# Opening of a two-block kernel: x loaded by feature columns instead of token rows, the first norm's sums made by TensorE and its factor multiplied in by GpSimd

## What is computed

```python
def rmsnorm(x, g):
    y = xf * lax.rsqrt(jnp.mean(xf * xf, axis=-1, keepdims=True) + RMS_EPS)
    return (y * g).astype(x.dtype)

cond = jax.nn.silu(c)
mod = (cond @ ada_w[i] + ada_b[i])[:, None, :]
sh1, sc1, g1, sh2, sc2, g2 = jnp.split(mod, 6, axis=-1)
h = rmsnorm(x, norm_mix[i]) * (1 + sc1) + sh1
qkv = h @ w_in
```

## Time and profile before

| | us |
|---|---|
| median of 3 runs | 2569.73 (2568.26 to 2569.94) |
| profiled execution, its own time | 2567.95 |
| span of the profiled execution | 2565.9 |
| PE busy | 2529.6 (99%) |
| DVE busy | 1970.2 (77%) |
| ACT busy | 1035.0 (40%) |
| POOL busy | 321.0 (13%) |

### The profile page before, as it was taken

The page is one execution under the profiler, slowest core; times in us unless marked ns, Lnnn a source line. Parts: engine busy times, 40 slices in busy tenths (PEclk is TensorE's granted clock), DMA queues, the critical chain, the costliest instruction groups (busy, mean ns, idle before and its releaser), DMA issues.

```text
span 2565.9 us, 37223 instructions
## 1 busy us (share of the span) xinstructions
PE 2529.6 (99%) x12662; PEld 2018.7 (79%) x12662; DVE 1970.2 (77%) x3476; ACT 1035.0 (40%) x1946; POOL 321.0 (13%) x454
## 2 busy tenths in 40 slices
PE   8999999999999999999999999999999999999998
PEld 6666688888888888777776888888888888878987
DVE  7888757889999889845555888998999987433566
ACT  6445725343333333454446453333333343111233
POOL 2011101000000000301111200000000017971000
PEclk9999999999999999999999999999999999999999
DMA  6333231211111111222322112121111132113122
GB/s 239 116 139 124 99 107 54 62 54 61 49 53 53 57 57 45 90 84 94 99 99 108 40 43 62 50 61 57 49 57 55 59 83 74 50 42 60 34 99 82
DMA packets 182017, 192.61 MB, mean 75 GB/s; under 512 B 18353, under 2 KB 146577, under 8 KB 181490
## 3 DMA queue, kind: packets, MB, share of 16 engines
q1 hardware_dynamic: 169954, 147.48, 18.0%
q0 software_dynamic: 11952, 43.65, 5.4%
HBM read 177.34 MB, written 12.58 MB: 74 GB/s over the span
## 4 chain that ended last, share of the span: by engine, by line
PE 93%; DVE 4%; ACT 2%; issue 1%; DMA 1%; POOL 0%; SPq 0%; DVEq 0%
PE psum L1423 21%; PE psum L1730 10%; PE psum L1731 10%; PE psum L1732 10%; PE psum L1500 5%; PE psum L1783 4%; PE psum L1782 4%; PE psum L1786 4%; PE psum L1502 4%; PE psum L1501 4%; PE psum L1771 3%; PE psum L1593 3%; PE psum L1621 3%; PE psum L1605 3%; DVE arena L2892 1%
## 5 line engine op out<-in xcount | busy, mean ns | idle before, releaser
L3181 DVE SCALAR_TENSOR_TENSOR xT<-psum,mod,xT 128x512 f32<-128x512 f32 x504 | 356.4, 745 | 61.6 <-PE psum L1786 61.3
L2346 ACT ACTIVATE w_high<-wpair 128x512 fp32r<-128x512 f32 x240 | 146.5, 626 | 315.8 <-DVE wpair L3113 244.9
L1423 PE MATMUL psum<-hT_high,w_low 128*128 128x512 f32 x928 | 261.0, 392 | 0.2 <-DVE arena L2888 0.2
L2549 ACT ACTIVATE arena<-arena 128x256 f32<-128x256 f32 (+3 forms) x296 | 146.6, 497 | 157.3 <-DVE arena L3451 157.1
L1500 PE MATMUL psum<-hT_high,w_low 128*128 128x512 f32 x480 | 203.0, 423 | 3.4 <-DVE h_low_mix L3630 3.2
L1423 PEld LDWEIGHTS psum<-hT_high,w_low 128*128 128x128 f32 x928 | 172.9, 188 | 38.3 <-issue 2.5
L1502 PE MATMUL psum<-hT_high,w_low 128*128 128x512 f32 x480 | 189.3, 394 | 0.0
L1501 PE MATMUL psum<-h_low_mix,w_low 128*128 128x512 f32 x480 | 188.5, 393 | 0.0
L1732 PE MATMUL psum<-hT_high,w_low 128*128 128x512 f32 x480 | 186.7, 389 | 0.0
L1730 PE MATMUL psum<-hT_high,w_high 128*128 128x512 f32 x472 | 183.6, 389 | 0.0
L1731 PE MATMUL psum<-h_low,w_high 128*128 128x512 f32 x472 | 183.6, 389 | 0.0
(11 more groups left out here) (450 smaller groups left out, 6257.5 us busy)
## 6 DMA issues: line engine op xcount, KB each, us to landing
wpair<-in_ffn_w_in_dram SPq DMA_DIRECT2D x176, 256.0 KB, 2.9
wpair<-in_ada_tiles_dram POOLq DMA_DIRECT2D x20, 1024.0 KB, 5.2
arena<-in_ffn_w_out_dram SPq DMA_DIRECT2D x80, 256.0 KB, 2.9
wpair<-in_ada_tiles_dram POOLq DMA_DIRECT2D x32, 512.0 KB, 3.6
wpair<-in_w_in_dram SPq DMA_DIRECT2D x24, 512.0 KB, 3.8
wpair<-in_b_tiles_dram SPq DMA_DIRECT2D x18, 512.0 KB, 3.3
arena<-in_ada_tiles_dram SPq DMA_DIRECT2D x8, 1024.0 KB, 15.6
wpair<-in_a_tiles_dram SPq DMA_DIRECT2D x12, 512.0 KB, 4.6
```

The lines of the kernel that those rows point to most:

```text
L1423: mm = nc.tensor.matmul(dst[:, HALF * a:HALF * a + HALF], w(k), src(k)[:, HALF * t:HALF * t + HALF], start=first and n == 0 and w is high ...
L2346: nc.scalar.activation(of_step(s, first_high, part_high)[name], part_raw[name], ACT.Copy).then_inc(part_high_ready, 1)
L2549: e = nc.scalar.activation(s, s, ACT.Exp, bias=stat_n[:, ti, h:h + 1], scale=-1.0, accum_out=stat_l[:, ti, h:h + 1])
L3181: nc.vector.scalar_tensor_tensor(xT[:, m, rows], psum[:, HALF * j:HALF * j + HALF], mod[:, l, 40 + m:41 + m], xT[:, m, rows], ALU.mult, AL ...
```

## The change

SP loads x from the host's transposed copy, one transfer for each feature chunk, into `x_raw` (the same 4 MB in the same order as the chunks are used), and loads the tile q1 behind the third pair of modulation rows. ACT squares whole chunks without a running sum, and the first half of the last chunk is squared by DVE. PE sums the squares: for each chunk 8 fp32 products of a 128x128 block of squares (stationary) with a column of ones. DVE and ACT make all 8 factors at once. PE runs 14 spare products, spreads the factors over all partitions (`factor_wide`, 8 products), and runs 26 more. ACT copies the spread factors to `r_wide`. POOL multiplies them into the chunks, except the first half of chunk 0, which is DVE's, and POOL makes the low parts of kv, q0 and q1 in between. The bias tables of unit 1 come behind that. ACT makes `hT_high` and `xT` both from `x_raw`. PE no longer transposes x; it issues chunks 0 to 4 of q1's products between the products of chunks 2 to 6, and transposes the values ahead of q1's last chunk.

```diff
-            for t in range(ST):
-                sp.dma_start(x_start[:, t, :], x[0, P * t:P * t + P, :]).then_inc(x_moved[t], 16)
+            for k in range(KC):
+                sp.dma_start(x_raw[:, k, :], x_columns[:, k, :]).then_inc(x_moved[k], 16)
...
-                if k in (1, 5):
+                if k in (1, 2):
                     load_mix("q0" if k == 1 else "q1", 0)
...
+            def scaled(k, first=0):
+
+                pool.wait_ge(x_moved[k], 16)
+                nc.gpsimd.tensor_tensor(x_raw[:, k, first:S], x_raw[:, k, first:S], r_wide[:, first:S], ALU.mult).then_inc(scaled_ready, 1)
+
             bias_tables(0)
+            tile_lows(("kv", 0))
+            pool.wait_ge(r_kept, 2)
+            scaled(0, HALF)
+            scaled(1)
+            tile_lows(("q0", 0))
+            scaled(2)
+            tile_lows(("q1", 0))
+            for k in range(3, KC):
+                scaled(k)
             bias_tables(1)
...
-                    if u == 0:
-                        for n in range(k + 2 if k else 0, min(k + 3, KC)):
-                            turn_x(n)
...
-                for k in range(KC):
-                    if k == 6:
+                    if 2 <= k < KC - 1:
+                        for half in range(2):
+                            project_chunk(u, "q1", half, k - 2, first_place("q1", half))
+                for k in range(5, KC):
+                    if k == KC - 1:
                         turn_values(u)
...
+            def square_sums(k):
+
+                pe.wait_ge(x_squared, k + 1 if k < KC - 1 else KC + 1)
                 for t in range(ST):
...
+                    mm = nc.tensor.matmul(psum[:, 3584 + t:3585 + t], square_place[k % 2][:, P * t:P * t + P], ones[:, :],
+                                          start=first, stop=k == KC - 1, skip_group_check=t > 0)
+                mm.then_inc(first_norm, 1)
+
+            def factor_wide():
+
+                pe.wait_ge(rstd_ready, RSTD_TURN[0])
+                for t in range(ST):
+                    mm = nc.tensor.matmul(r_spread[:, P * t:P * t + P], rst[:, 0, 4, t:t + 1].to_broadcast([P, P]), ident[:, :],
+                                          start=True, stop=True)
+                mm.then_inc(first_norm, 1)
...
-                spare_products(12)
...
             spread_row()
+            for k in range(KC):
+                square_sums(k)
+            pe.wait_ge(const_ready, 6)
+            spare_products(14, psum[:, 2560:2816])
+            factor_wide()
+            spare_products(26, psum[:, 2560:2816])
+            pe.wait_ge(cond_ready, 3)
             attention(0, 4)
...
+            def square_chunk(k, first=0):
+
+                act.wait_ge(x_moved[k], 16)
+                if k >= 2:
+                    act.wait_ge(first_norm, k - 1)
+                nc.scalar.activation(square_place[k % 2][:, first:S], x_raw[:, k, first:S], ACT.Square).then_inc(x_squared, 1)
...
+            act.wait_ge(first_norm, KC + 1)
+            for half in range(2):
+                cols = slice(HALF * half, HALF * half + HALF)
+                nc.scalar.activation(r_wide[:, cols], r_spread[:, cols], ACT.Copy).then_inc(r_kept, 1)
             for k in range(KC):
                 act.wait_ge(gg_ready, k + 1)
...
+                act.wait_ge(scaled_ready, k + 1)
+                shift_, gain_ = mod[:, 0, k:k + 1], gain[:, 0, k:k + 1]
+                nc.scalar.activation(hT_high[:, k, :], x_raw[:, k, :], ACT.Identity, bias=shift_, scale=gain_)
+                nc.scalar.activation(xT[:, k, :], x_raw[:, k, :], ACT.Identity, bias=shift_, scale=gain_).then_inc(shifted, 1)
+                if k < 2:
+                    tile_highs((("q0", "q1")[k], 0))
...
+            dve.wait_ge(first_norm, KC)
+            nc.vector.tensor_scalar(var[:, 0, :], psum[:, 3584:3584 + ST], 1.0 / D, EPS, ALU.mult, ALU.add).then_inc(var_ready, 1)
+            dve.wait_ge(dev_ready, 1)
+            reciprocal_root(0).then_inc(rstd_ready, 1)
...
+                    if k == 0 and b == 0:
+                        dve.wait_ge(r_kept, 1)
+                        nc.vector.tensor_tensor(x_raw[:, 0, 0:HALF], x_raw[:, 0, 0:HALF], r_wide[:, 0:HALF], ALU.mult)
...
-                if k == 0:
-                    tile_lows(("kv", 0))
-                else:
+                if k > 0:
                     first_low(k - 1)
-                if k == 1:
-                    tile_lows(("q0", 0))
```

More of the change, by code:

```diff
@@ L557, in two_blocks_kernel @@
         x_squared = sem("x_squared")
+        first_norm = sem("first_norm")
+        r_kept = sem("r_kept")
         scaled_ready = sem("scaled_ready")
@@ L1148, in bias_tables, with tile_lows @@
                     nc.gpsimd.tensor_scalar(lay["bias"][:, u % 2, h, 0:w], src[:, 0:w], -a.slope[h], None, ALU.mult).then_inc(bias_ready, 1)
+            def tile_lows(name):
+                whole, high, low = tile_parts(name)
+                pool.wait_ge(tile_high, SPLITS.index(name) + 1)
+                pool.wait_ge(tile_split, SPLITS.index(name))
+                nc.gpsimd.tensor_tensor(low, whole, as_f32(high), ALU.subtract).then_inc(tile_split, 1)
+            def scaled(k, first=0):
+                pool.wait_ge(x_moved[k], 16)
+                nc.gpsimd.tensor_tensor(x_raw[:, k, first:S], x_raw[:, k, first:S], r_wide[:, first:S], ALU.mult).then_inc(scaled_ready, 1)
             distances(LAY[0]["dist"], LAY[0]["bias"][:, 0, 0, :], -P, P)
             bias_tables(0)
+            tile_lows(("kv", 0))
[7 more added lines that the diff above has]
+                scaled(k)
             bias_tables(1)
@@ L1175, in half_tile_low @@
                     ins.then_inc(tile_split, 1)
[L1177 to L1182, removed]
             def sink_difference(t):
@@ L1539, in project_halves @@
                         project_chunk(u, "q1", half, k, first_place("q1", half))
-            def turn_x(k):
-                dst, ready = take(("xn", k))
-                pe.wait_ge(scaled_ready, ST)
+            def square_sums(k):
+                pe.wait_ge(x_squared, k + 1 if k < KC - 1 else KC + 1)
                 for t in range(ST):
-                    mm = nc.tensor.transpose(dst[:, P * t:P * t + P], x_start[:, t, P * k:P * k + P], ident[:, :])
-                mm.then_inc(ready, 1)
+                    first = k == 0 and t == 0
+                    mm = nc.tensor.matmul(psum[:, 3584 + t:3585 + t], square_place[k % 2][:, P * t:P * t + P], ones[:, :],
[7 more added lines that the diff above has]
+                mm.then_inc(first_norm, 1)
             def spread_row():
@@ L2634, in _ @@
+            for k in range(KC - 1):
+                square_chunk(k)
+            square_chunk(KC - 1, HALF)
+            act.wait_ge(var_ready, 1)
+            nc.scalar.activation(dev[:, 0, :], var[:, 0, :], ACT.Sqrt).then_inc(dev_ready, 1)
             tile_highs(("kv", 0))
+            act.wait_ge(first_norm, KC + 1)
+            for half in range(2):
+                cols = slice(HALF * half, HALF * half + HALF)
+                nc.scalar.activation(r_wide[:, cols], r_spread[:, cols], ACT.Copy).then_inc(r_kept, 1)
@@ L2635, in _ @@
             for k in range(KC):
                 act.wait_ge(gg_ready, k + 1)
[L2637 to L2641, removed]
-                if k == 0:
-                    tile_highs(("q0", 0))
+                act.wait_ge(scaled_ready, k + 1)
@@ L3598, in _ @@
             nc.vector.tensor_copy(cond, psum[:, 0:D]).then_inc(cond_ready, 1)
[L3599 to L3624, removed]
+            dve.wait_ge(x_moved[KC - 1], 16)
+            dve.wait_ge(first_norm, KC - 1)
+            last = x_raw[:, KC - 1, 0:HALF]
+            nc.vector.tensor_tensor(square_place[1][:, 0:HALF], last, last, ALU.mult).then_inc(x_squared, 1)
+            dve.wait_ge(first_norm, KC)
+            nc.vector.tensor_scalar(var[:, 0, :], psum[:, 3584:3584 + ST], 1.0 / D, EPS, ALU.mult, ALU.add).then_inc(var_ready, 1)
+            dve.wait_ge(dev_ready, 1)
+            reciprocal_root(0).then_inc(rstd_ready, 1)
             dve.wait_ge(cond_ready, 3)
```

22 lines of the change are left out of this document (7 added, 15 removed).

## The result

The kernel after takes 2610.97 us (median of 4 runs, 2609.07 to 2611.54), against 2569.84 us for the kernel before on the same chip (2568.26 to 2570.94). The ratio is 1.0159 [1.0142, 1.0177]. The forecast was 2589.7 us with a range of 2570 to 2605: the sign was right, the size was half of the real one, and the time lies 6 us above the range. The profiled execution of the kernel after took 2609.07 us.

A forecast was written before the change was run, and what follows sets the result against it. PE bounds the kernel (93% of the chain), so the opening costs what it delays the first scores: +19.9 us on the profiled 2567.95 gives 2587.9, plus 1.8 to the median, 2589.7 us; range 2570 to 2605.

The forecast's parts named there:

- Step 1: PE's sums of squares: low rate for the first 5.3 us, then 1.82 us a chunk, ending at 24.9 us.
- The first rival: PE slow through all the sums, to 36.8 us, spare products 2.7 us longer: +14.6 us, 2604.3 us; chance 0.12.
- Step 2: Factor hidden behind 14 spare products (5.6 us), then a spread of 1.95 us; DVE goes on at 33.1 us.
- Step 3: DVE's turns of 3.74 us a chunk put the last gain at 60.1 us, +10.7 us against 49.42.
- Step 4: GpSimd beside DVE: colliding SBUF reads cost DVE 1.7 us an operation, 16.2 us in all; last gain 76.3 us.
- Step 5: Last gain to first scores: split done 79.8 us, PE 0.9 us behind, then 7.2 us; scores 87.9 us, +19.9.
- Costed at nothing: Opening's transposes, low-clock first products, unit 1's bias tables, later modulation rows and ACT's extra SBUF pass: no added time.
- the full lock: POOL operations beside DVE in the opening each cost it their full length, 22.6 us in all: 6.4 us above the forecast.

The follow-up runs named there:

- Experiments 1 and 3: Against the changed kernel: 1 put the 14 spare products ahead of the sums, 2610.4 us; 3 streamed squares past ones as weights, output not the reference's, 2596.9 us.
- Experiment 5: All of POOL's two-operand work in the opening (multiplications, three weight low parts) moved to DVE, against the changed kernel; 2599.8 us.
- kernels 6: The 16 first dot products read the condition from PSUM instead of SBUF, against the changed kernel; 2600.4 us.
- kernel 9: Against the changed kernel: DVE adds squares before PE sums, condition read from PSUM, three gains ahead of the factor, POOL's multiplications released by DVE's steps; 2575.8 us.

## Why the prediction was wrong, step by step

In the prediction's own chain, from 68.04 us before to the first scores:

| step | forecast, us | measured, us | missed by |
|---|---|---|---|
| 1, sums end | 24.9 | 36.2 | +11.3 |
| 2, DVE goes on | 33.1 | 46.6 | +2.2 |
| 3 and 4, last gain | 76.3 | 94.3 | +4.5 |
| 5, first scores | 87.9 | 108.1 | +2.2 |

(The last column is what each step adds.)

- **Step 1 failed, and it is more than half of the error.** It said that PE is slow "at first" and took the 5.3 us of the old spare products, then the fast rate of the earlier trace rows. Those rows stand in a long stretch of 512-column products at the full clock; in after the clock never rises during the sums (0.214 us a record to the end, against 0.113 in the earlier trace rows). Experiments 1 and 3 show both halves of that. The first rival, with 36.8 us, was right and had 0.12. Its evidence was in the prediction: no row showed such a stretch start from the low clock. That was a reason to give it the larger chance.
- **Step 2** had the right mechanism and a spread of the right length (1.95 us). The 28 records of the spare products took 7.95 us, not 5.6, as they were the ones to bring the clock back (39.7 us). The rival had priced just this, at 2.7 us.
- **Step 3** held. In after itself the last turn, with POOL done, is 3.74 us (the gains start at 90.37 and 94.11). Experiment 5 shows it from the other side: without POOL's work a chunk costs DVE 4.7 us with its multiplication of 1.14 in it (gains at 71.0, 75.7, 80.5, 85.2).
- **Step 4** had the right mechanism and a term too small. The waits of DVE sum to 94.3 - 46.6 - 27.0 (step 3's own length) = 20.7 us against 16.2. I had doubled the 0.85 us of the earlier trace rows for twice the columns. It is about 2.1 us each: the instruction waits out all of what POOL has left. The earlier trace rows don't show less than that; I misread them. Their 0.85 us was lost beside POOL operations that take 1.04 us alone, not "1.0 to 1.3":

```profile
2272.09 1.04 POOL L1356 TENSOR_TENSOR arena<-arena 128x512 f32<-128x512 f32 x1
```

  In after the one POOL operation of 512 columns takes 1.28 us and costs the dot product beside it 1.0 us (2.29 instead of 1.27), and one of 1024 columns, 2.38 us alone, costs 2.1:

```profile
47.11 1.28 POOL L1162 TENSOR_TENSOR arena<-arena 128x512 f32<-128x512 f32 x1 [7.11 <-ACT arena L2649]
```

```profile
47.18 2.29 DVE L2906 CUSTOM_DVE_ANT_0 arena<-arena,vec 128x1024 f32<-128x1024 f32 x1
```

  In all three it is POOL's own length less 0.2 to 0.3 us; doubling 0.85 doubled the part that isn't lost as well, and took an operation for twice 1.04 us that lasts 2.38. The Trainium skill, "SBUF — State Buffer", section "Who interferes with whom", has a DVE instruction with two SBUF inputs and a GpSimd instruction that reads SBUF exclude each other for the whole instruction. With this the trace agrees: the one-column gain takes 2.17 us instead of 0.16, and a dot product with its second operand in PSUM doesn't wait at all. Of the 22.6 us forecast by that rule some 19.8 came, in nine waits of 2.0 to 2.1 us and one of 1.0.
- **Step 5** was short by 2.2 us. It counted 0.9 us of lag for PE, over turns of 3.74 us, in which PE has 18 products, 4.1 us at the 0.23 us of the chain. But the last split comes only 2.5 us behind the one before it (95.4 and 97.9 us). In the trace 41 products start between the last split and the first scores; 30 of them are those that the forecast counted, so PE was 11 products, 2.5 us, behind, not 0.9. The rest is small: 0.2 us for 0.2275 us a product instead of 0.22, and some 0.4 us of handoffs. The stretches at the low clock have no part in it: they end at 80.7 us, and PE still stood idle for 1.3 us ahead of chunk 3's products at 83.6.
- **Costed at nothing**: the later modulation rows and the transposes were right; the shift at the first scores was kept within 0.3 us up to 2149 us. The bias tables were not quite free: beside them, from 81.0 us, two dot products take 1.51 us instead of 1.27 and two gains 0.33 instead of 0.16, 0.8 of the 20.7 us of step 4.
- **The range** had each upper bound alone. Slow sums and the full lock together are 2589.7 + 14.6 + 6.4 = 2610.7 us, close to the 2611.0 measured. Nothing made them exclude each other, and neither a rival nor the range held both. That the sum fits so closely is luck: the two terms are 3.0 us too large (14.6 against the 13.5 of steps 1 and 2, 6.4 against 4.5), and step 5 (2.2) and the later norm (1.6) fill that up.

## What to carry to other kernels

A rate taken from a stretch where PE was kept busy by wide products need not hold for the same instruction at the head of a kernel; look for rows that start from the low clock. Here adding first on an idle engine brought the first scores 12.8 us earlier, and the form of the sum that streams 512 columns 12.5, without the turn that it would still need. Before work is moved to GpSimd, list the DVE instructions beside it that read two SBUF operands, and count one whole GpSimd instruction for each meeting, also for those of one column; reading one side from PSUM, or releasing GpSimd at the right step, takes it away. And where a transformation turns a per-tile dependency into one on all of the input, the first product's time is its price, even when the work taken off is real.

## What the runs showed that I had not expected

**A half-clock stretch two milliseconds later.** All ten kernels with the change (after and the nine experiments) spend more in the later norm, which none of them touches. From the start of its one-column sums to the start of its spread it is 10.4 us before, 12.0 in eight of the ten (after: 2188.7 to 2200.8) and 13.6 in two. The table by stretches, after and then before:

```profile
2188.70:2192.30 3.60, 3.60 (x34) 1.00 0.49 146
2193.50:2196.90 3.40, 3.40 (x10) 0.50 0.00 0
```

```profile
2148.90:2152.40 3.50, 3.50 (x34) 1.00 0.50 150
2152.40:2160.00 7.60, 7.60 (x39) 1.00 0.01 2
```

1.2 us behind the same 3.6 us of sums the clock falls in one kernel and not in the other, with PE busy throughout. That costs 1.6 us, or 3.2 in kernels 6 and 9, where the clock falls while the sums still run (they take 4.83 and 4.23 us instead of 3.63). It is 3.2 of the 7.2 us by which the span of kernel 9 exceeds that of before. Why the kernel before is spared wasn't settled: only one profile of it was read, and no run changed that place alone.

**The wait takes no account of DVE's size.** A gain of one column waits as long (2.0 us) as a dot product of 1024 (2.1); what sets the wait is the length of POOL's instruction.
